# The opening of a three-block network on one core: low parts ahead of squares, a first tile by quarters, and a reordered start of the S5 steps

## The reference, cut to what matters

```python
def rmsnorm(x, g):
    return x * lax.rsqrt(jnp.mean(x * x, axis=-1, keepdims=True) + RMS_EPS) * g

def s5_layer(h, ...):
    u, z = jnp.split(rmsnorm(h, g_pre) @ w_in, 2, axis=-1)
    y = s5_ssm(u, ...)               # Re(C h_t) + D u_t,  h_t = Abar h_{t-1} + Bbar u_t
    y = jax.nn.gelu(y)
    y = y * jax.nn.sigmoid(y @ w_glu + b_glu)
    return h + rmsnorm((y * jax.nn.silu(z)) @ w_out, g_post)
```

## Time and profile before

| | |
|---|---|
| time, median of 3 runs | 3070.48 us (3069.7 to 3071.14) |
| profiled execution, its own time | 3066.98 us |
| its span from first to last instruction | 3065.2 us |
| PE busy | 2982.9 us, 97% of the span |
| POOL, DVE, ACT busy | 1639.3, 1360.0, 1187.9 us |
| weight tiles loaded, 1 MB each | 223 |

### The profile page before, as it was taken

The page is one execution under the profiler, slowest core; times in us unless marked ns, Lnnn a source line. Parts: engine busy times, 40 slices in busy tenths (PEclk is TensorE's granted clock), DMA queues, the critical chain, the costliest instruction groups (busy, mean ns, idle before and its releaser), DMA issues.

```text
span 3065.2 us, 53484 instructions
## 1 busy us (share of the span) xinstructions
PE 2982.9 (97%) x21192; PEld 2376.1 (78%) x21192; DVE 1360.0 (44%) x2166; ACT 1187.9 (39%) x1640; POOL 1639.3 (53%) x1355
## 2 busy tenths in 40 slices
PE   7899999999899999999999999999999999998997
PEld 5778888888788888888888878777777777775686
DVE  8788861120443132222322046456456455466612
ACT  5455653243533232323333254343343343344521
POOL 4455544454777777777773464444444444344342
PEclk9999999999999999999999999999999999998998
DMA  4566673242222222222222242222222222225522
GB/s 171 171 198 203 204 205 149 96 151 96 70 90 93 95 89 86 89 100 88 89 86 91 98 149 97 82 104 77 85 106 73 90 98 80 91 77 162 167 96 96
DMA packets 128935, 347.97 MB, mean 114 GB/s; under 512 B 61936, under 2 KB 65008, under 8 KB 98304
## 3 DMA queue, kind: packets, MB, share of 16 engines
q1 hardware_dynamic: 128784, 345.73, 33.7%
HBM read 306.07 MB, written 35.55 MB: 111 GB/s over the span
## 4 chain that ended last, share of the span: by engine, by line
PE 49%; issue 25%; POOL 20%; DVE 4%; ACT 2%; DMA 1%; SPq 0%; POOLq 0%; DVEq 0%; ACTq 0%
POOL wlo L173 16%; PE bank L196 14%; PE bank L198 14%; PE bank L197 14%; POOL g L2001 2%; PE bank L1408 1%; PE bank L1390 1%; PE bank L2106 1%; POOL wk L644 1%; PE bank L1399 1%; PE bank L2180 0%; DMA wraw<-in_wall_dram 0%; PE bank L2146 0%; POOL wk L638 0%; ACT whi L168 0%
## 5 line engine op out<-in xcount | busy, mean ns | idle before, releaser
L173 POOL TENSOR_TENSOR wlo<-wraw,whi 128x512 fp32r<-128x512 f32 (+1 forms) x896 | 1181.5, 1349 | 1171.8 <-ACT whi L168 1171.7
L196 PE MATMUL bank<-rhi,whi 128*128 128x512 f32 x3632 | 1455.9, 401 | 42.8 <-POOL wlo L173 28.0
L197 PE MATMUL bank<-rlo,whi 128*128 128x512 f32 x3632 | 1419.6, 391 | 0.0
L198 PE MATMUL bank<-rhi,wlo 128*128 128x512 f32 x3632 | 1419.1, 391 | 0.0
L196 PEld LDWEIGHTS bank<-rhi,whi 128*128 128x128 f32 x3632 | 683.8, 188 | 217.2 <-issue 40.2
L198 PEld LDWEIGHTS bank<-rhi,wlo 128*128 128x128 f32 x3632 | 684.0, 188 | 145.8
L197 PEld LDWEIGHTS bank<-rlo,whi 128*128 128x128 f32 x3632 | 684.9, 189 | 136.9 <-issue 4.3
L168 ACT ACTIVATE whi<-wraw 128x2048 fp32r<-128x2048 f32 (+2 forms) x227 | 428.2, 1887 | 450.7 <-PE bank L198 272.2
L1182 POOL TENSOR_TENSOR wraw<-wraw,vec 128x512 f32<-128x512 f32 x248 | 252.1, 1047 | 0.0
L961 DVE TENSOR_TENSOR ssum<-ssum,wk 128x512 f32<-128x512 f32 x28 | 20.6, 737 | 278.1 <-ACT wk L951 278.1
L2001 POOL TENSOR_TENSOR g<-g,wk 128x256 f32<-128x256 f32 x80 | 58.8, 757 | 108.9 <-PE bank L1774 57.5
(11 more groups left out here) (385 smaller groups left out, 3056.1 us busy)
## 6 DMA issues: line engine op xcount, KB each, us to landing
wraw<-in_wall_dram SPq DMA_DIRECT2D x223, 1024.0 KB, 4.9
g<-in_bmat_dram SPq DMA_DIRECT2D x16, 512.0 KB, 3.9
g<-scr_e SPq DMA_DIRECT2D x128, 64.0 KB, 3.0
scr_a<-ssum SPq DMA_DIRECT2D x24, 256.0 KB, 2.3
g<-in_xp_dram SPq DMA_DIRECT2D x4, 1024.0 KB, 11.8
g<-in_cmat_dram SPq DMA_DIRECT2D x16, 256.0 KB, 7.0
scr_u<-wk SPq DMA_DIRECT2D x16, 256.0 KB, 2.6
scr_y<-wk SPq DMA_DIRECT2D x16, 256.0 KB, 3.2
```

Source lines behind the costliest of these rows:

```text
L173: ins = pool.tensor_tensor(wlo[:, slot, c], wraw[:, slot, c], whi[:, slot, c].bitcast(F32), ALU.subtract)
L196: pe.matmul(out[:, :], whk, rhi[:, k, :], start=(k == first), stop=False)
L197: pe.matmul(out[:, :], whk, rlo[:, k, :], start=False, stop=False)
L198: ins = pe.matmul(out[:, :], wlk, rhi[:, k, :], start=False, stop=(k == last))
```

## The change

It has six parts, all in the first 140 us:

1. **Low parts ahead of squares.** `split_hi` and `split_lo` of the first norm no longer carry the squares. ACT makes its 16 rhi first, then squares 0 to 7, whi of tile 2, squares 8 to 15 (`first_squares`), the root, whi of tile 3, and then the two sines. DVE makes its 16 rlo, then the 16 additions.
2. **First tile by quarters.** POOL signals each quarter of tile 0's wlo, and PE waits for the quarter.
3. **Third tile in its own bank, norm later.** PE runs tile 0, tile 1, the norm's sum, tile 2 into `banks[6]`, tile 3. DVE scales z tiles one place earlier: 0 and 1 directly after the reciprocal (1 into `ub[1]`), 2 and 3 where 1 and 2 stood; `exp_by_hand` moves behind the first two.
4. **Powers ahead of tables on DVE.** In step 0, `ub` and the power come ahead of `dve_out`.
5. **Tiles ahead of kernels on PE.** In steps 1 and 2 the tile's products come ahead of L541, and in step 1 ACT makes whi of tile 7 ahead of copying the kernel out.
6. **Loads reordered on SP.** In step 0 the load of tile 7's weights and the read of u come ahead of the powers' store.

```diff
@@ sp_step, j = 0
                 if lo == 0:
+                    w_load_after(sp, u_tile(0, 0) + 3, 0, u_tile(0, 0) + 3)
+                    ug_load(sp, 0, 0)
                     sp.wait_ge(e_rdy, E_STEPS)
@@ dve_step
-            if u == 0:
+            if u == 0 and lo > 0:
                 z_scale(d, h + 3, 3 * h + 3, 1)
...
-            if lo == 0:
-                dve_out(d, link, (j, u))
             if hi <= 15:
                 d.wait_ge(gemm, u_tile(u, h) + 1 - u)
...
                     state_powers(d, link, (4,))
                     d.sem_inc(e_rdy, 6)
+                    dve_out(d, link, (j, u))
@@ pe_step
+            if lo in (1, 2):
+                project(pe, u_tile(u, h), 0)
             if lo >= 1 and hi <= 16:
...
-            if hi <= 16:
+            if hi <= 16 and lo not in (1, 2):
                 project(pe, u_tile(u, h), 0)
@@ act_step
+            if lo == 1:
+                act.wait_ge(gemm, u_tile(u, h))
+                make_hi(act, u_tile(u, h) + 1, 0, slot_order(0, j + 3))
             if lo >= 1 and hi <= 16:
                 act.wait_ge(k_mm, t + 1)
@@ parameters
-            z_scale(d, 1, 1, 1)
+            z_scale(d, 2, 2, 0, of=banks[6])
...
-                    z_scale(d, 2, 2, 0)
+                    z_scale(d, 3, 3, 1)
@@
+        def first_squares(act, ks):
+
+            for k in ks:
+                wait(act, ssq, k - 1)
+                act.activation(sqb0[k % 2], g1[:, k * T:(k + 1) * T], ACT.Square).then_inc(sq_f, 1)
@@ pool
-            for n in range(EARLY + 1):
+            pool.wait_ge(w_hi, 1)
+            for q in range(4):
+                ins = pool.tensor_tensor(wlo[:, 0, quarter(q)], wraw[:, 0, quarter(q)],
+                                         whi[:, 0, quarter(q)].bitcast(F32), ALU.subtract)
+                ins.then_inc(w_lp if q < 3 else w_lo, 1)
+            for n in range(1, EARLY + 1):
                 make_lo(pool, n, n % 2)
@@ act
-            split_hi(act, g1, V_G1, 0, (sqb0, 0), landed=(x_part, 16), ks=range(13, KT))
+            split_hi(act, g1, V_G1, 0, landed=(x_part, 16), ks=range(13, KT))
+            first_squares(act, range(0, 8))
+            act.wait_ge(gemm, 1)
+            make_hi(act, 2, 0, slot_order(0, 1))
+            first_squares(act, range(8, KT))
+            norm_root(act, V_EPS6, st_mm, 1)
@@ dve
-            split_lo(d, g1, V_G1, 0, (sqb0, 0))
+            split_lo(d, g1, V_G1, 0)
+            for k in range(KT):
+                add_square(d, sqb0, 0, k)
             angle(d, link)
-            exp_by_hand(d, link, p_am, p_x, p_n, p_f)
             norm_recip(d, link, 0)
             z_scale(d, 0, 0, 0)
+            z_scale(d, 1, 1, 1, to=ub[1])
+            exp_by_hand(d, link, p_am, p_x, p_n, p_f)
             parameters(d, link)
@@ pe
-            project(pe, 0, 0, wait_r=0)
+            project(pe, 0, 0, wait_r=0, parts=LP_FIRST)
+            project(pe, 1, 1)
             norm_sum(pe, 0)
-            for n in range(1, EARLY):
-                project(pe, n, n % 2)
+            project(pe, 2, 0, to=banks[6], held=2)
+            project(pe, 3, 1)
```

More of the change, by code:

```diff
@@ L310, in slot_order, with z_store, z_scale, z_silu @@
             return i - (4, -4)[slot]
-        def z_store(sp, j):
+        def z_store(sp, j, of=zt):
             sp.wait_ge(z_rdy, j + 1)
-            sp.dma_start(scr_z[j], zt).then_inc(z_wr, 16)
-        def z_scale(d, j, n, slot):
+            sp.dma_start(scr_z[j], of).then_inc(z_wr, 16)
+        def z_scale(d, j, n, slot, of=None, to=None):
             d.wait_ge(gemm, n + 1)
-            wait(d, z_wr, 16 * j)
-            d.tensor_tensor(zt, acc[slot][:, :], rstd[:, :], ALU.mult).then_inc(evac, 1)
-        def z_silu(act, n, out=None):
+            if to is None:
+                wait(d, z_wr, 16 * j)
+            d.tensor_tensor(zt if to is None else to, acc[slot][:, :] if of is None else of, rstd[:, :],
+                            ALU.mult).then_inc(evac, 1)
+        def z_silu(act, n, out=None, of=zt):
             act.wait_ge(evac, n + 3)
-            act.activation(zt if out is None else out, zt, ACT.Silu).then_inc(z_rdy, 1)
+            act.activation(of if out is None else out, of, ACT.Silu).then_inc(z_rdy, 1)
         def registers(eng, *values):
@@ L337, in w_load_after, with c_load, ug_load @@
             w_load(sp, n, slot)
+        def c_load(sp, j):
+            sp.wait_ge(q_rdy, j + 1)
+            sp.dma_start(m["cq"], a["cmat"][j + 1]).then_inc(cq_in, 16)
+        def ug_load(sp, j, u):
+            wait(sp, yq, j - 1)
+            sp.wait_ge(u_wr, 16 * j + 16)
+            sp.dma_start(ug[u], scr_u[j].rearrange("s (c g) k -> (s c) (g k)", g=GT)).then_inc(ug_in[u], 16)
         def sp_step(sp, j, u, h, lo, hi):
@@ L379, in sp_step @@
                     sp.dma_start(tv[s * SC:(s + 1) * SC, :, s * SC:P], kv[:, :, 0:P - s * SC]).then_inc(t_in, 16)
[L380 to L383, removed]
+            if hi <= 15 and lo > 0:
+                ug_load(sp, j, u)
             if lo >= 2 and hi <= 17:
@@ L386, in sp_step @@
                 sp.dma_start(scr_y[j - 2].rearrange("s (c g) k -> (s c) (g k)", g=GT), m["yg"]).then_inc(yg_wr, 16)
-            if hi <= 15:
+            if hi <= 15 and lo > 0:
                 w_load_after(sp, u_tile(u, h) + 3, 0, u_tile(u, h) + 3 - u)
             if hi <= 14:
-                sp.wait_ge(q_rdy, j + 1)
-                sp.dma_start(m["cq"], a["cmat"][j + 1]).then_inc(cq_in, 16)
+                c_load(sp, j)
             if lo == 15:
@@ L611, in act_step @@
                 z_silu(act, 3 * h + 3)
-            if hi <= 16:
+            if hi <= 16 and lo != 1:
                 n = u_tile(u, h) + 2 - u
@@ L615, in act_step @@
                 make_hi(act, n, 0, slot_order(0, j + 3))
-            else:
+            elif lo == 17:
                 z_silu(act, 28)
@@ L1361, in fox_first @@
             n = N_GATE + 1
-            project(pe, n, 1, range(0, 12), held=N_GATE, parts=0)
+            project(pe, n, 1, range(0, 12), held=N_GATE, parts=LP_FOX)
             norm_sum(pe, 2)
-            project(pe, n, 1, range(12, KT), parts=0)
+            project(pe, n, 1, range(12, KT), parts=LP_FOX)
             project(pe, n + 1, 0, to=banks[6], held=N_GATE)
@@ L2473, in _ @@
             act.activation(pre["v8"], p_abs, ACT.Sin, bias=vec[:, V_HPI:V_HPI + 1], scale=-1.0).then_inc(pa_sc, 1)
-            norm_root(act, V_EPS6, st_mm, 1)
-            for n in range(EARLY - 1):
-                act.wait_ge(gemm, n + 1)
-                make_hi(act, n + 2, n % 2, slot_order(n % 2, n // 2 + 1))
-                z_silu(act, n)
+            z_silu(act, 0)
+            z_silu(act, 1, of=ub[1])
+            act.wait_ge(gemm, 3)
+            make_hi(act, 4, 0, slot_order(0, 2))
+            z_silu(act, 2)
             steps(act, act_step, link, 4)
```

10 lines of the change are left out of this document (6 added, 4 removed).

## The result

The changed kernel takes 3080.17 us (median of 8 runs, 3074.64 to 3083.68) against 3070.36 us before: 1.0035 times, interval 1.0027 to 1.0044. It is slower by some 10 us. The forecast was 3078.5, in a range of 3066 to 3085.

A forecast was written before the change was run, and what follows sets the result against it. PE bounds the kernel, with DVE second in the opening. An earlier start (-5.0) and exposed squares (+9.7) give +5.2 at tile 5, steps 1 and 2 raise it to +8: 3078.5 us from median 3070.48, range 3066 to 3085.

The forecast's parts named there:

- The start: Tile 0 by quarters: PE's first matmul comes about 5.0 us earlier, at about 15.5.
- -5.0 (start) + 9.7: Opening's sum: PE's earlier start and squares in the open together bring +5.2 us at tile 5.
- 72.0 + 10.4 + 5.1: Tile 5's start: pw_rdy 1, then POOL's powers, then tile 5's low part, giving 87.5 instead of 82.25.
- Whatever makes DVE later by more than that shows on PE: Before tile 5: PE waits only 0.79 us, so any larger DVE delay in the opening reaches PE.
- Low parts beside POOL: First norm on DVE: rlo locked beside POOL start 1.71 us apart, free ones 0.66; the last ends at 31.7.
- The additions rode free in POOL's turn: First norm: beside POOL, a rlo alone costs DVE as much as a rlo and an addition together.
- The additions in the open: After the low parts: 16 additions at 0.79 us plus 1.4 take 14.0; the sum is ready at 45.7 against 36.02.
- The gain of part 4: Step 0 on DVE: powers return at 106.0 instead of 112.5; the 6.5 us gain is hidden behind the kernel's chain.
- Steps 1 and 2: Tiles ahead of the kernel's matmuls leave x's chain uncovered; the delay grows from +5.2 to +8 (+4 to +10).
- the locks of POOL's low parts 6 and 7 against these chains, 1 to 2 us each at two places: Steps 1 and 2: DVE slowed beside POOL, raising the half of tile 8's delay from 5.7 to 8 us.
- worse: Rival: granted clock falls after each new idle stretch and coefficients are locked; +13.6, 3084 us, chance 0.12.
- Loads, put at 0: SP's reordered loads in step 0 cost 0, at most a few us, hidden by the chain through the copies.

The follow-up runs named there:

- e4: Kernel before with only part 2, tile 0's low part signalled by quarters; 3073.62 us, 1.0010 times the kernel before.
- e1: Changed kernel, but POOL holds back tile 1's low part until DVE has made all 16 low parts of x; 3083.23 us, 1.0042 times the kernel before.
- e9: Changed kernel with POOL's tile 1 low part after all low parts of x, and the norm's sum inside tile 1; 3075.46 us, 1.0023 times before.
- e12: Kernel before with parts 4 to 6, but SP issues the powers' store ahead of tile 7's weights and u; 3076.11 us, 1.0016 times before.
- e7: Kernel before with parts 4 and 6, and step 1's kernel matmuls inside tile 6 behind its tenth block; 3077.65 us, 1.0019 times before.
- e2: Kernel before with parts 1 to 3 of the change alone; 3082.89 us, 1.0034 times the kernel before.
- e3: Kernel before with parts 4 to 6 of the change alone; 3076.27 us, 1.0019 times the kernel before.
- e8: Kernel before with part 4, kernel's matmuls inside tiles 6 and 7, SP storing powers before tile 7's weights and u; 3068.36 us, 0.9997 times before.
- e13: Opening of before, steps 0 to 2 rearranged for DVE, kernel's copies ahead of u's store, SP's old order in step 0; 3072.56 us, 1.0005 times before.

## Why the prediction was right, and where its sizes were off

- **The start.** Forecast 15.5, measured 15.89; worth nothing by itself, as e4 shows. So the sum's "-5.0 (start) + 9.7" is not what makes +5.2 at tile 5. That figure came from 72.0 + 10.4 + 5.1, which holds.
- **What DVE may be late.** "Whatever makes DVE later by more than that shows on PE", by more than 0.79, was a misreading: POOL began the powers 5.2 us after pw_rdy 1. The forecast of tile 5 has this slack in it all the same, since it counts from 72.0 and not from PE's wait.
- **Low parts beside POOL.** Forecast 31.7 for the last, measured 32.0, and e1 shows the four locked ones at 1.0 us each. "The additions rode free in POOL's turn" is shown where POOL ran: beside it a rlo alone starts every 1.70 us now, and a rlo with its addition did so every 1.68 to 1.70 before. That holds for seven of the 16 additions; the first two lay in a wait for x.
- **The additions in the open.** Forecast 14.0, measured 14.2; the sum at 45.7 forecast, 46.18 measured. They were not all free before: the other seven, with POOL quiet, made a pair start every 1.26 us where a rlo alone starts every 0.66, about 4.2 us together. What their move costs DVE is therefore about 10 us.
- **pw_rdy 1 and tile 5.** Forecast 72.0 and 87.5, measured 72.99 and 88.55. Here the chain over DVE and POOL is shown to be the loss: e9 takes 4.9 us off DVE's sum, lets the norm through, and tile 5 follows by 7.7.
- **The gain of part 4.** It is hidden behind the kernel's chain, as forecast (7.59 us of DVE waiting for ACT); e12 shows for parts 4 to 6 alone that the chain, not the store, ends last there.
- **Steps 1 and 2: the term that was too small.** The forecast came from +5.2 at tile 5 to "+8" at half of tile 8; measured are +6.3 and +11.9. Of "the locks of POOL's low parts 6 and 7 against these chains, 1 to 2 us each at two places" one came as sized, the coefficients of step 1 with 5.4 instead of 4.07. The other was larger: dve_out of step 1 took 8.7 instead of 5.3, and the turns and scans behind it on DVE are what y waited 2.12 for. And the low clock after the new idle stretches, which I had kept for the rival "worse", is in it: 19.3 - 16.1 = 3.2 us behind the wait before tile 5.
- **Loads, put at 0.** Right for parts 4 to 6 alone (e12), but by little. In the changed kernel SP stores the powers at 97.28 and reads them back from 104.65, 7.4 later instead of 3.0, and in e7, without the kernel's chain, the store beside tile 7's weights and the coefficients beside its low part make x just as late.
- **The total.** Median + 9.8 measured, + 8 forecast. That they lie so close is partly luck: at the landmark the loss is 12.5, beyond the + 4 to + 10 of the sum, and the interval of the time reaches from + 8.3 to + 13.5.

That the two halves of the change cost about 10 and 6 us apart is measured (e2, e3). What remains open is why e4 is 0.1% above before, why the halves add up to more than the whole, and how much of the last 1 to 2 us between e2 and the whole change is real: their intervals overlap.

## What to carry to other kernels

Before work is moved out from between two instructions to let the second one start earlier, ask what the second was waiting for: here seven of the 16 additions stood in a time that DVE would have spent waiting for POOL anyway, and moving all of them behind the low parts made DVE about 10 us later. Then ask what the late engine is waited for, and since when: here POOL was busy for the first 5.2 us of that. An earlier first matmul is worth nothing if the last input ends the tile, and a chain that is laid behind a tile stands open unless other work covers it. Where DVE is as full as PE, removing one wait shows the next; judge an order by DVE's chain to the end of the stretch, not by the wait it removes.

## What the runs showed of the hardware that was not expected

- The same seven instructions of the input coefficients took 4.1 us with POOL quiet (e8, 99.9 to 104.0) and 8.4 us beside a low part of POOL (e7): an earlier load of weights, by bringing POOL's work forward, slowed DVE's. The Trainium skill, "SBUF — State Buffer", section "Who interferes with whom", has the exclusive lock behind this; that it is reached through a DMA's place in a queue is what the runs add.
- A 512 KB store issued behind a 1 MB load and a 256 KB read let SP go on 7.4 us later (e7, 90.22 to 97.59; the changed kernel has the same 7.4). It took 3.0 alone (before, 93.33 to 96.29) and 3.6 with the same two transfers issued right behind it (e8, 89.24 to 92.79). In e13, behind a 256 KB store and a 512 KB load issued within 1.6 us ahead of it, it took 5.8 (87.72 to 93.47). In these runs the price goes with what was issued just ahead of the store.
